# Tiles of xT 1088 bytes apart in place of 1024, in a two-block transformer kernel on one core

## What is computed

```python
def first_block(x, ...):
    x = layer_norm(alpha * x + 0.5 * swiglu(x, ffn_w_gate[l, 0], ffn_w_up[l, 0], ffn_w_down[l, 0]), ...)
    x = layer_norm(alpha * x + hybrid_mixer(x, w_in[l], ...), ...)
    x = layer_norm(alpha * x + 0.5 * swiglu(x, ffn_w_gate[l, 1], ffn_w_up[l, 1], ffn_w_down[l, 1]), ...)

def second_block(x, p, ...):
    u = rmsnorm(h, norm_mix_pre[i])
    ... = jnp.split(u @ w_in[i], offs, axis=-1)      # gated delta rule and sparse attention follow
    h = h + rmsnorm(mixed, norm_mix_post[i])
    f = rmsnorm(h, norm_ffn_pre[i]) @ w_up[i]
    f = causal_dwconv(f, conv_ffn[i]) + conv_ffn_b[i]
    f = (jax.nn.gelu(f_gate) * f_val) @ w_down[i]
    h = h + rmsnorm(f, norm_ffn_post[i])
    e = (p[i] @ w_ple[i]) * jax.nn.sigmoid(h @ w_ple_gate[i])
    h = h + rmsnorm(e, norm_ple_post[i])
```

## Time and profile before

| | |
|---|---|
| median of 3 runs | 1219.23 us |
| lowest and highest | 1214.09, 1222.84 us |
| profiled execution, own time | 1235.01 us |
| its span, first to last instruction | 1233.2 us |
| mean granted clock of TensorE | 0.96 |
| PE, PEld busy | 92%, 85% |
| POOL, ACT, DVE busy | 74%, 51%, 40% |

### The profile page before, as it was taken

One profiled execution on the slowest core, in us unless ns is written; L12 is line 12 of the kernel. 1 busy time (PEld: TensorE's weight loads), 2 busy tenths in 40 slices (PEclk: granted clock), 3 DMA queues, 4 the chain that ended last, 5 costly groups with the idle time before them and its releaser, 6 DMA issues.

```text
span 1233.2 us, 22532 instructions
## 1 busy us (share of the span) xinstructions
PE 1135.4 (92%) x8040; PEld 1053.6 (85%) x8040; DVE 487.8 (40%) x978; ACT 626.1 (51%) x1009; POOL 908.5 (74%) x700
## 2 busy tenths in 40 slices
PE   6999997998999898999996997999799979999975
PEld 6999996997888887999995987889688879999964
DVE  3211117103346548311116439734564164344462
ACT  5444444444557745444444754454455474554554
POOL 7999995997552685999995697383225869899963
PEclk9999998999998998999998899899899989999988
DMA  8866563675332353666564455152124546656541
GB/s 288 291 185 188 191 184 112 187 204 159 117 104 69 109 185 134 203 194 192 194 189 154 121 190 168 52 154 69 59 62 123 179 144 186 182 189 185 188 134 52
DMA packets 52631, 193.40 MB, mean 157 GB/s; under 512 B 5840, under 2 KB 6096, under 8 KB 51920
## 3 DMA queue, kind: packets, MB, share of 16 engines
q1 hardware_dynamic: 50976, 184.57, 48.0%
q10 hardware_dynamic: 1584, 7.81, 1.8%
HBM read 191.31 MB, written 1.05 MB: 156 GB/s over the span
## 4 chain that ended last, share of the span: by engine, by line
POOL 43%; PE 28%; issue 24%; DVE 2%; ACT 2%; POOLq 1%; ACTq 0%; DVEq 0%
POOL weights_low L479 43%; PE banks L510 16%; PE acc L510 9%; PE banks L908 2%; ACT tmp L1254 1%; PE banks L703 0%; ACT prob L1139 0%; POOLq L482 0%; DVE xs L1583 0%; DVE xs L1577 0%; DVE nmx L1627 0%; DVE sS L1624 0%; PE banks L592 0%; ACT L1095 0%; POOLq L476 0%
## 5 line engine op out<-in xcount | busy, mean ns | idle before, releaser
L479 POOL TENSOR_TENSOR weights_low<-ring,weights_high 128x512 fp32r<-128x512 f32 x696 | 908.3, 1335 | 304.6 <-ACT weights_high L1033 301.0
L510 PE MATMUL banks<-xT_high,weights_high 128*128 128x256 f32 x1680 | 480.8, 286 | 16.2 <-POOL weights_low L479 11.3
L1033 ACT CAST weights_high<-ring 128x1024 fp32r<-128x1024 f32 x348 | 362.0, 1048 | 232.4 <-PE banks L510 157.5
L510 PE MATMUL banks<-xT_low,weights_high 128*128 128x256 f32 x1680 | 475.6, 283 | 0.0
L510 PE MATMUL banks<-xT_high,weights_low 128*128 128x256 f32 x1680 | 475.2, 283 | 0.0
L510 PEld LDWEIGHTS banks<-xT_high,weights_high 128*128 128x128 f32 x1680 | 323.1, 192 | 21.2 <-issue 12.0
L510 PEld LDWEIGHTS banks<-xT_low,weights_high 128*128 128x128 f32 x1680 | 323.7, 193 | 2.4
L510 PEld LDWEIGHTS banks<-xT_high,weights_low 128*128 128x128 f32 x1680 | 325.4, 194 | 0.0
L1464 DVE TENSOR_TENSOR hf<-act_buf,banks 128x256 f32<-128x256 f32 x44 | 18.5, 421 | 275.8 <-ACT act_buf L1059 275.8
L510 PE MATMUL acc<-weights_high,hT_high 128*128 128x512 f32 x264 | 104.9, 397 | 4.9 <-DVE hT_low L1473 4.9
L510 PE MATMUL acc<-weights_low,hT_high 128*128 128x512 f32 x264 | 104.9, 397 | 0.0
(11 more groups left out here) (316 smaller groups left out, 1463.6 us busy)
## 6 DMA issues: line engine op xcount, KB each, us to landing
ring<-in_stream SPq DMA_DIRECT2D x348, 512.0 KB, 3.7
rows<-in_big_rows ACTq DMA_DIRECT2D x3, 1024.0 KB, 6.9
rows<-in_big_rows ACTq DMA_DIRECT2D x3, 512.0 KB, 5.2
cst<-in_consts ACTq DMA_DIRECT2D x1, 1411.0 KB, 9.2
gates<-in_x_fm SPq DMA_DIRECT2D x2, 512.0 KB, 5.3
xs<-in_x_tm ACTq DMA_DIRECT2D x1, 1024.0 KB, 6.1
out<-xs SPq DMA_DIRECT2D x4, 256.0 KB, 2.0
pT<-in_p_fm ACTq DMA_DIRECT2D x1, 256.0 KB, 5.0
```

What stands on the lines that cost most here:

```text
L479: last = nc.gpsimd.tensor_tensor(wlo[:, slot, hs], ring[:, slot, hs], whi[:, slot, hs].bitcast(F32), ALU.subtract)
L510: ins = nc.tensor.matmul(o, lhsT, rhs, start=start, stop=stop, **kw)
L1033: nc.scalar.copy(whi[:, ch % RING, :], ring[:, ch % RING, :]).then_inc(S["hi_ready"], 1)
```

## The change

Both fillers go. The four small tensors stat, nmx, den and coef stand ahead of xT in place of behind it. xT is allocated with 272 words a tile, of which the first 256 are used, so its tiles lie 1088 bytes apart. No instruction changes but in its addresses.

```diff
@@ -305,15 +305,13 @@
         srow = sb("srow", [N_SROW])
         xs = sb("xs", [2, 2, D])
         res = sb("res", [2, D])
-        sb("fill_x", [88])
-        xT = pair("xT", [KD, T])
         stat = sb("stat", [64])
         nmx = sb("nmx", [2, 2])
         den = sb("den", [2, 2])
         coef = sb("coef", [2, 2])
+        xT = tuple(half[:, :, 0:T] for half in pair("xT", [KD, T + 16]))
         tmp = sb("tmp", [2, 2 * T])
 
-        sb("fill_stage", [168])
         hT = pair("hT", [GROUP, T], in_ffn)
         hf = sb("hf", [2, T], in_ffn)
         act_buf = sb("act_buf", [2, 2 * T], in_ffn)
```

## The result

The changed kernel takes 1239.45 us (median of 4 runs, 1237.64 to 1242.38) against 1219.89 us before (4 runs, 1214.09 to 1222.84). The ratio is 1.0142 with a 95% interval of 1.0108 to 1.0175: 19.6 us slower. The forecast was 1216 us in a range of 1204 to 1231, so it missed in sign and in range. The ratios in this document leave out the two executions of before that took over 1.5% more than its fastest: the first profiled one (1235.01 us) and one of 1235.41 us among the later runs. The profiled execution of after takes 1242.38 us with a span of 1240.6 us.

What follows compares the result with a forecast made beforehand. PE was taken to bound the long stretches, through matmul count times start-to-start distance. The streams' 3.0 us, with nothing for other terms, came off the timed median of 1219.2 us: 1216 us, range 1204 to 1231.

Steps and rivals of the forecast that it cites:

- the writers of xT: Instructions writing xT tiles: no cost taken; the two four-tile copies at the start, were each 10% dearer, would add 0.2 us.
- The two gaits: In the xT matmuls on PE: start-to-start distances of 117.9 ns (long) or 113.4 ns (short), each lasting hundreds of matmuls.
- The streams: The 5040 matmuls streaming xT: skewed tiles would average 115.6 ns against 116.2, saving 3.0 us, the whole expected effect.
- the rcs matmuls: Compression matmuls streaming 256 weight columns against rcs, tiles 120 bytes apart: 34 steps at 115.6 ns each, taken as nearest row.
- The caution beside it: On the compression matmuls: only 30 columns are loaded, so a load meets the stream for less time; no size given.
- The short gait is lost: Rival, chance 0.15: 64 bytes a tile make load and stream meet in each projection; 6.1 to 13.0 us more, 1225 to 1232.
- The sum: Whole kernel: 3.0 us off the profiled span and off the timed runs' median of 1219.2, giving 1216 us.
- Gait from history, not from address: Rival, chance 0.16: same code and addresses run at both paces, so the change does nothing, 1219 us.
- the position k makes no difference: Within xT: all eight tiles of a group keep its pace, leaving no room for a slow or fast tile.
- Release: Rival, chance 0.22: moving the address 64 bytes every three matmuls leaves 113.4 ns holding; 9.7 to 16.6 us less, 1203 to 1210.
- Floor removed: Rival, chance 0.03: 113.4 ns comes from equal places and spread tiles go below; bounded at 47 us, 1172 us.
- The sign in the weight loads: Load of weights_low on PE: 192 ns when xT matmuls pace at 117.9 ns, 188 ns at 113.4.

Runs made afterwards that it cites:

- second trace of before: The kernel before, unchanged, profiled a second time: 1222.23 us, span 1220.4, mean pace of xT matmuls 114.2 ns.
- the first map: Matmuls alone, no block computed: sixteen fixed xT stand-ins 64 bytes apart, plus tiles 1024 or 1088 bytes apart; paces 113.3 to 120.0 ns.
- the last kernel: The changed kernel, tiles still 1088 bytes apart, with the first begun 112 bytes past the weights' place modulo 256: 1241.11 us, ratio 1.0146 to before.
- distance 0: The kernel before with xT, tiles 1024 bytes apart, begun at the weights' own place modulo 256: 1247.05 us, ratio 1.0189.
- the finer map: Matmuls alone again: sixteen fixed places 16 bytes apart, tile pitches 1024 to 1280 bytes, and weights streamed against loaded x; xT-type paces 113.3 to 120.0 ns.
- the kernel at 112: The kernel before with all xT tiles, 1024 bytes apart, begun 112 bytes past the weights' place modulo 256: 1217.26 us, ratio 0.9959.

## Why the prediction was wrong

**What held.** PE alone sets the time of the long stretches and its steps are all that the change can alter; no instruction was added; the writers of xT cost nothing (ACT's copies of four tiles take 1044 and 1045 ns in after as in before, its writes of one tile 552); the moved small tensors cost nothing that can be measured (ratio 1.0012 with the move alone); the clock was the same (1.00 in the sorted stretches). The two gaits are real and differ between stages and between executions, which the second trace of before shows outright.

**The term that failed: "The streams".** It took the pace of skewed tiles from the rcs matmuls, 115.6 ns, and came to -3.0 us. Measured, the pace is 117.75 ns, and the xT steps cost 16.7 us where 3.0 were to be gained. The rcs row was the nearest in that its distances change from step to step, but it loads 30 columns where xT's groups load 128, it steps by other distances, and there it is the loaded side that moves. The caution beside it, that a load then meets the stream for less time, should have moved the estimate: if a meeting of load and stream sets the long gait, a row with a quarter of the load can only bound the pace from below. That the smaller load is what made the row too fast is argued here; no run varied the columns loaded.

**The base was wrong too.** The sum started from the first profile's mean of 116.2 ns, and was then set off from the median of the runs. The text noticed that the runs may be shorter in gait than the profiled execution, and used this only so as not to count a gain twice. It also meant that a loss had to be counted from 114.2: the rival of the lost gait was priced at 6.1 to 13.0 us, 1225 to 1232, and from a base of 114.2 it comes to 5040 x (117.9 - 114.2) = 18.6 us, 1238 us, against the 1239.45 measured. A profiled execution that lies 15.8 us above the median was an outlier, in good part by its gaits (9.2 of the 12.8 us to the second profile), and its gaits were no sample of the others. How long the timed runs were in each gait is not on record, since a run without a profile has no steps; 114.2 is the second profile's.

**"The short gait is lost", given 0.15, is what happened.** Its argument was that all fast groups stood at one distance of 64 bytes between xT and weights. The rows did not single that out, since all slow groups stood at the same one; but the conclusion held: of four distances, 64 bytes apart, it is the only one that can run at 113.3, and the skew puts three tiles in four on the other three. By the first map the four average (120.0 + 117.8 + 118.7 + 113.3 or 117.8) / 4, 117.5 to 118.6; after has 117.75. That this fits is partly chance, as the tiles taken one by one do not keep these paces, and the same average missed by 1.5 ns for the last kernel.

**"Gait from history, not from address", given 0.16, was half right,** and the half misled. At before's place something other than the address decides between 113.3 and 117.8. The inference from one address pattern with two gaits to "address does not matter" does not follow; nor does "the position k makes no difference", since in before all k have one and the same distance. These rows were silent about other distances.

**"Release", given 0.22,** would need the short gait at changing distances. The map, after and the last experiment all have the reverse. **"Floor removed", given 0.03,** did not occur: no steady pace went below 113.3. The estimate of 35 us by the Trainium skill, "TensorE: Matmul & The Clock Gate", section "Wait — 56ns, not 53.3ns?", whose rule gives 109.2 ns for 256 columns, would need a pace that no place of the two maps has.

**The sign in the weight loads did not hold.** The load of weights_low at 192 ns was to mark the long gait. In after it is at 188 with matmuls of 279 to 281.

**The page that speaks of ports.** The rows of the maps show a pace between 113.3 and 120.0 ns with nothing changed but the place of what streams, and whole kernels between 1222 us (before) and 1247 us (distance 0). The Trainium skill, "SBUF — State Buffer", section "Who interferes with whom", has the two read ports of PE independent, which the prediction took to mean that places would not matter. The measurement disagrees with that reading, and decides; whether it is at the ports that the time is lost, no run here shows.

**What stays open.** Why the period is 256 bytes, and what meets what inside PE's reading, is not shown. Nor is it shown that it is the distance to the weights that counts and not the streaming tile's own place, since no weight block was moved under a fixed stream. That the loaded side's place matters as well is shown by the sections of the finer map with x loaded and weights streamed (226.7 to 233.5 ns, last section below). What picks the gait of a stage in one execution is not known, nor why the clock was at its lower level for less time in the kernel at 112. hT, mT, yT and oT were not moved.

## What to carry to other kernels

Where PE is busy without a gap and its paces come in two sizes, look at the distance between the moving tile and the weight block modulo 256 bytes and measure the pace at each place in a kernel of matmuls alone. Then keep all tiles at one place that the map has as fast, with equal pitches that are multiples of 256 bytes, not spread ones: a walk over several places was slow even where the first one was fast. Before a change to such a kernel is costed, take a second profile of it; a profiled execution well off the median can have another mix of gaits, and both gains and losses are then counted from the wrong base. Compare the time at each clock level as well before a gain of a few us is put down to a pace. A row with a smaller load than the case in question is at best a bound for it, not an estimate.

## What the runs showed of the hardware beyond what was expected

- With 128 columns loaded and 256 streamed, and the weights at one place, the steady pace depends on the distance of the two operands modulo 256 bytes: 120.0 ns at 0, 117.8 at 64, 113.3 at 112, 118.7 at 128 (120.0 in one section of sixteen), 113.3 or 117.8 at 192.
- Two more places, 16 and 144, showed both a short and a long pace as 192 does; 112 showed only the short one as its steady pace.
- The short pace is entered slowly: after five steps of 118.4 ns in the mean at 192, after ten of 118.3 at 112 (54 groups each, second trace of before and the kernel at 112).
- When the tiles walk over several places, a tile's pace is not its place's: 114.0 and 117.2 ns for two tiles at 192 in after, 119.7 and 118.8 for two tiles at 112 in the last kernel.
- With the roles exchanged, x loaded and 512 columns of weights streamed, two sections each: 226.7 ns with x at distance 0, 228.9 and 229.0 at 192, 233.3 and 233.4 at 64, 232.4 and 233.5 at 128.
- Before's runs spread over 19 us (1216.53 to 1235.41 in 19 runs, one of them above 1229.45). Part of a spread is the clock: the same 241 matmuls took 38.2 us in one execution at a mean granted clock of 0.91, and 34.2 in another at 1.00.
